# Feed-forward of a two-block layer on one core: ScalarE multiplies the modulation weights in place, GpSimd only adds

## The reference

```python
mod = c_act @ w_ada[l] + b_ada[l]                      # one row of six pieces: sh1, sc1, gt1, sh2, sc2, gt2
...
h = _rmsnorm(x, norm2_g[l]) * (1.0 + sc2) + sh2
x = x + gt2 * _conv_ffn(h, w_up[l], conv_w[l], conv_b[l], w_down[l])     # conv of width 3, silu(gate) * val
...
mod = jnp.einsum('bd,de->be', jax.nn.silu(c), w_ada[layer]) + b_ada[layer]    # second block
```

## Time and profile before

| | |
|---|---|
| median of 3 runs | 3269.93 us (3267.48 to 3271.69) |
| the profiled execution's own time | 3266.9 us |
| its span | 3265.1 us |
| feed-forward in the span | about 1011 to 1844 us |
| PE busy in the span | 2618.0 us (80%) |
| DVE busy | 2094.0 us (64%) |
| ACT busy | 1069.4 us (33%) |
| POOL busy | 672.6 us (21%), all but a little of it in the feed-forward |

### The profile page before, as it was taken

The page is one execution under the profiler, slowest core; times in us unless marked ns, Lnnn a source line. Parts: engine busy times, 40 slices in busy tenths (PEclk is TensorE's granted clock), DMA queues, the critical chain, the costliest instruction groups (busy, mean ns, idle before and its releaser), DMA issues.

```text
span 3265.1 us, 50408 instructions
## 1 busy us (share of the span) xinstructions
PE 2618.0 (80%) x22384; PEld 2536.3 (78%) x22384; DVE 2094.0 (64%) x2395; ACT 1069.4 (33%) x1155; POOL 672.6 (21%) x371
## 2 busy tenths in 40 slices
PE   1189911149497999999999659999999999999986
PEld 1179901149496999999999548999899999999986
DVE  5736488874546888777788645555644576576443
ACT  1133210012233333333333244434433344344332
POOL 0000000000005887887888200000000000000000
PEclk6589955569698999999999879999999999999998
DMA  7746558830256677677777325555466665666653
GB/s 258 241 118 182 160 173 286 288 123 4 62 155 169 208 225 232 212 223 235 226 232 233 103 58 142 143 158 148 137 185 186 181 168 166 183 161 163 181 157 102
DMA packets 757608, 568.64 MB, mean 174 GB/s; under 512 B 45680, under 2 KB 643824, under 8 KB 757264
## 3 DMA queue, kind: packets, MB, share of 16 engines
q1 hardware_dynamic: 756624, 562.40, 59.1%
q0 software_dynamic: 768, 3.02, 0.3%
HBM read 563.29 MB, written 2.10 MB: 173 GB/s over the span
## 4 chain that ended last, share of the span: by engine, by line
PE 71%; DVE 20%; issue 3%; ACT 3%; POOL 1%; DMA 1%; SPq 0%; DVEq 0%; ACTq 0%; POOLq 0%
PE bank L556 19%; PE bank L558 19%; PE bank L557 19%; DVE acc L1309 9%; PE bank L733 2%; PE bank L546 2%; PE bank L610 1%; PE bank L584 1%; PE bank L586 1%; PE bank L585 1%; DVE ez L1713 1%; DVE w_low L1269 1%; DVE hid_low L1607 1%; ACT hf L1003 1%; PE bank L775 1%
## 5 line engine op out<-in xcount | busy, mean ns | idle before, releaser
L556 PE MATMUL bank<-act_high,w_high 128*128 128x256 f32 x4608 | 1314.7, 285 | 123.5 <-issue 56.4
L557 PE MATMUL bank<-act_low,w_high 128*128 128x256 f32 x4608 | 1309.3, 284 | 0.0
L558 PE MATMUL bank<-act_high,w_low 128*128 128x256 f32 x4608 | 1309.0, 284 | 0.0
L1269 DVE TENSOR_TENSOR w_low<-ring,w_high 128x2048 fp32r<-128x2048 f32 x388 | 933.6, 2408 | 433.0 <-ACT w_high L973 426.1
L556 PEld LDWEIGHTS bank<-act_high,w_high 128*128 128x128 f32 x4608 | 888.3, 193 | 128.5 <-issue 59.6
L973 ACT ACTIVATE w_high<-ring 128x2048 fp32r<-128x2048 f32 x388 | 737.6, 1903 | 477.3 <-DMA ring<-w_up 235.9
L557 PEld LDWEIGHTS bank<-act_low,w_high 128*128 128x128 f32 x4608 | 888.4, 193 | 0.1
L558 PEld LDWEIGHTS bank<-act_high,w_low 128*128 128x128 f32 x4608 | 887.9, 193 | 0.1
L515 POOL TENSOR_SCALAR prod<-adf,cact 128x512 f32<-128x512 f32 x165 | 362.9, 2199 | 54.7 <-DMA adf<-w_ada 39.5
L546 PE MATMUL bank<-con,acc 128*128 128x1 f32 x288 | 57.1, 319 | 345.5 <-DVE small L1314 345.5
L546 PEld LDWEIGHTS bank<-con,acc 128*128 128x128 f32 x288 | 55.3, 286 | 348.7 <-DVE small L1314 348.7
(11 more groups left out here) (370 smaller groups left out, 2821.4 us busy)
## 6 DMA issues: line engine op xcount, KB each, us to landing
ring<-w_in SPq DMA_DIRECT2D x182, 1024.0 KB, 5.8
ada<-w_ada SPq DMA_DIRECT2D x100, 1024.0 KB, 5.1
ring<-w_up SPq DMA_DIRECT2D x88, 1024.0 KB, 6.0
adf<-w_ada SPq DMA_DIRECT2D x44, 1024.0 KB, 8.1
ring<-w_down SPq DMA_DIRECT2D x44, 1024.0 KB, 5.0
ring<-w_out SPq DMA_DIRECT2D x16, 1024.0 KB, 6.1
ring<-w_mla SPq DMA_DIRECT2D x16, 1024.0 KB, 5.2
ring<-w_o SPq DMA_DIRECT2D x16, 1024.0 KB, 6.0
```

Of the source, the lines that this page charges most:

```text
L556: pe.matmul(o, wh, ah, start=first, stop=False, skip_group_check=True)
L557: pe.matmul(o, wh, al, start=False, stop=False, skip_group_check=True)
L558: return pe.matmul(o, wl, ah, start=False, stop=last, skip_group_check=True)
L1269: v.tensor_tensor(WL[s][:, 0:WIDE[n]], ring[s][:, 0:WIDE[n]], f32(WH[s][:, 0:WIDE[n]]), ALU.subtract)\
```

## The change

ScalarE multiplies each row tile of a quarter in place, in the `adf` buffer, two tiles behind each up unit's copy: tiles 0 and 1 of quarter q behind up 2q+2 (behind its silu), tiles 2 and 3 behind up 2q+3; those of quarter 3 behind up 0 and up 1 of the next iteration. A new semaphore `f_scaled` counts tiles. GpSimd waits for a quarter's four tiles and then only adds: the first two tiles plus the last two (1024 columns at once), then the two halves, then into the accumulator. It still signals `f_free` when it is done. `prod2` is gone.

```diff
+        f_scaled = sem("f_scaled")
...
                 for q in range(4):
                     k = 4 * turn + q
-                    pool.wait_ge(f_landed[k % 2], 16 * (k // 2 + 1))
-                    w = AF[k % 2][:, :].rearrange("p (j n) -> p j n", j=4)
-                    for j in range(4):
-                        c = (0 if turn < 4 else DT) + 4 * q + j
-                        col = cact[:, c:c + 1]
-                        if q == j == 0:
-                            ins = pool.tensor_scalar(acc[:, :], w[:, j, :], col, None, ALU.mult)
-                        else:
-
-                            pool.tensor_scalar(prod2[:, :], w[:, j, :], col, None, ALU.mult).then_inc(pool_seq, 1)
-                            pool.wait_ge(pool_seq, B.up("pool_seq"))
-                            ins = pool.tensor_tensor(acc[:, :], prod2[:, :], acc[:, :], ALU.add)
...
+                    pool.wait_ge(f_scaled, 4 * (k + 1))
+                    w = AF[k % 2]
+                    pool.tensor_tensor(w[:, 0:1024], w[:, 0:1024], w[:, 1024:2048], ALU.add).then_inc(pool_seq, 1)
+                    pool.wait_ge(pool_seq, B.up("pool_seq"))
+                    if q:
+                        pool.tensor_tensor(w[:, 0:512], w[:, 0:512], w[:, 512:1024], ALU.add).then_inc(pool_seq, 1)
+                        pool.wait_ge(pool_seq, B.up("pool_seq"))
+                        ins = pool.tensor_tensor(acc[:, :], w[:, 0:512], acc[:, :], ALU.add)
+                    else:
+                        ins = pool.tensor_tensor(acc[:, :], w[:, 0:512], w[:, 512:1024], ALU.add)
+                    ins.then_inc(f_free, 1)
+                    pool.wait_ge(f_free, k + 1)
...
+            def scaled(k, js):
+
+                turn, q = divmod(k, 4)
+                act.wait_ge(f_landed[k % 2], 16 * (k // 2 + 1))
+                for j in js:
+                    w, c = AF[k % 2][:, 512 * j:512 * j + 512], (0 if turn < 4 else DT) + 4 * q + j
+                    act.activation(w, w, ACT.Copy, scale=cact[:, c:c + 1]).then_inc(f_scaled, 1)
+
             for i in range(12):
                 for k in range(8):
...
                     if k % 2 == 0 and (k or i):
                         finish()
+                    if 8 * i + k >= 2 and 4 * i + k // 2 - 1 < 44:
+                        scaled(4 * i + k // 2 - 1, (0, 1) if k % 2 == 0 else (2, 3))
```

More of the change, by code:

```diff
@@ L210, in program @@
         acc2 = [at(f"acc2{b}", W0 + 106 + 2 * b, [P, 512]) for b in range(2)]
-        prod2 = at("prod2", W0 + 70, [P, 512])
         BH = at("mix_high", W0 + 32, [P, 8, T], F32R)
```

## The result

The changed kernel takes 3526.45 us (median of 4 runs, 3519.26 to 3527.59), the kernel before 3268.7 us in the same series: a ratio of 1.078, 95% interval 1.077 to 1.080. The forecast was slower, 3487 us, range 3445 to 3525; the direction and the mechanism hold, and the measured median lies 1.5 us past the upper end. The profiled execution took 3525.5 us, 258.6 us more than that of before.

What follows compares the result with a forecast made beforehand. PE was taken to set the pace. Nine iterations at +20.3 us (183 us), +13 us in the first period and +21 us in the last made 217 us on 3266.9, 3484, plus 3 for the median: 3487 us, range 3445 to 3525.

Steps and rivals of the forecast that it cites:

- The walk: One feed-forward iteration step by step from up 3's end as 0: 94.8 us against 74.5, +20.3 us, nine times.
- quarter 2 issued: On SP's queue: quarter 2's load goes at 5.8 us, after quarter 0's adds, up 6's and up 7's loads right behind.
- PE's first wait: Before up 6: PE could begin at 11.5 us but `w_low` is ready at 20.2, a wait of 8.7 us.
- quarter 3 issued: On SP's queue: quarter 3's load goes at 29.6 us, after quarter 1's adds, the next up 0 and up 1 behind.
- PE's second wait: Before the next up 0: PE is done at 34.4 us, `w_low` comes at 43.9, a wait of 9.5 us.
- half clock after it: After the second wait PE starts at the lower clock level, 1.2 GHz in place of 2.4: 2.7 us charged.
- wait before the first down unit: PE's wait for `hid_low`: shorter than the present 3.1 us because `w_low` is no longer slow, 1.3 us.
- The first period: The stretch up to the first of the nine iterations, 81.5 us before, shorter by what it already lost: +13 us.
- the last: The last iteration: down unit at 51.6 us after up 3 in place of 30.8, its weights behind quarter 3: +21 us.
- The wide add: GpSimd's add of 1024 columns: taken as 2.6 us, within bounds of 1.28 and 2.6 us.
- Faster: Rival: the `hid_low` wait (36.0 us) and its half clock (19 us) go, SP's delay is covered: 3212 us, 4 in 100.
- Worse: Rival: up 6 lands with up 7 and POOL's adds each fall behind a `w_low`, 27 us: 3560 us, 7 in 100.

Runs made afterwards that it cites:

- Runs 1, 3 and 4: The changed kernel with, in turn: quarter loads later on SP's queue (3302.64 us), multiplies one pair of units sooner (3297.52 us), a third quarter buffer (3305.68 us).
- Run 7: The changed kernel with one GpSimd wait added, so quarters 2 and 3 are added beside the down units: 3458.83 us, ratio 1.059.
- b_no_pool_work: The kernel before the change with GpSimd's multiplies and adds left out: 3211.13 us, ratio 0.983.
- a_late_defer: The changed kernel with quarter loads later on SP's queue and GpSimd's adds of quarters 2 and 3 beside the down units: 3234.11 us, ratio 0.990.
- a_no_adds: The changed kernel with GpSimd's adds left out and both orders kept: 3359.03 us, ratio 1.029.

## Why the prediction was right, and where its sum was off

**The mechanism** was that quarter 2's and quarter 3's loads wait on SP's in-order queue for a buffer that ScalarE's late multiplies keep from GpSimd, with the weights of up 6, up 7 and the next up 0 and up 1 behind them. Runs 1, 3 and 4 take that wait away in three ways and get 221 to 229 us back.

**The walk**, from up 3's end (1527.8 in the iteration shown), forecast and measured:

| step | forecast | measured |
|---|---|---|
| quarter 2 issued | 5.8 | 5.8 |
| from its issue to the split of up 6 | 10.0 | 8.8 |
| PE's first wait | 8.7 | 7.3 |
| quarter 3 issued | 29.6 | 28.0 |
| from its issue to the split of the next up 0 | 10.0 | 8.8 |
| PE's second wait | 9.5 | 8.3 |
| up 0 begins | 43.9 | 41.1 |
| half clock after it | 2.7 | 1.7 (its copy came at 1576.42, 7.5 us later) |
| wait before the first down unit | 1.3 | 5.9 |
| half clock after that | 0 | 2.3 (1588.07 to 1596.15) |
| the iteration | 94.8 | 98.0 (mean of nine: 98.6) |

The copies of up 3 at 1134.59 and 2022.05 us are nine iterations apart: 98.6 us each, +24.1 in place of +20.3, nine times 217 us. The first period cost 17.2 (1134.59 - 1117.42; forecast 13) and the last 22.5 us (the down unit at 2075.40, 53.4 after its up 3, against 30.8; forecast 21). Together 257 of the 258.6 us between the two profiled executions.

**The step that failed** is the last point of the walk: "a wait before the first down unit. That one gets shorter, since `w_low` is no longer slow and was done long ago: 1.3 us". It became 5.9 us with 2.3 us of half clock, 6.9 us more than forecast and past the 3.5 us that its range allowed, while all up to up 0's begin was 2.8 us shorter and the half clock after it 1.0 us. These errors pull against each other, so that 3487 us came as near as it did in part by luck: with the rest of the walk exact, 6.9 us in each of ten iterations would have made it some 70 us too low. The chain of waits ahead of that unit, in the changed kernel:

```profile
1572.94 2.67 DVE hid_low L1611
...
1575.63 1.28 DVE sil L1599
...
1576.93 1.48 DVE sil L1600
...
1582.66 0.43 DVE hfu L1606
...
1585.33 2.61 DVE hid_low L1611
1587.93 0.14 issue
1588.07 0.55 PE bank L550
```

and what GpSimd did in that time:

```profile
1572.90 2.41 POOL L508 TENSOR_TENSOR adf<-adf 128x1024 f32<-128x1024 f32 x1 [17.12 <-ACT adf L1112]
1575.39 1.36 POOL L511 TENSOR_TENSOR adf<-adf 128x512 f32<-128x512 f32 x1
1576.83 1.30 POOL L513 TENSOR_TENSOR acc<-adf,acc 128x512 f32<-128x512 f32 x1
1585.29 2.35 POOL L508 TENSOR_TENSOR adf<-adf 128x1024 f32<-128x1024 f32 x1 [7.17 <-ACT adf L1112]
```

Each of these two wide adds begins 0.04 us before a `hid_low`. GpSimd is released by ScalarE's last two multiplies, which end at 1572.76 and 1585.15 us; `hid_low` stands behind a `w_low` that ends 0.3 us after them, just too late, and takes 2.6 us where alone it takes 0.42. The loss is 2.2 + 0.9 + 1.0 + 2.2 = 6.3 us for an iteration. Run 7 shows it: with the adds elsewhere 67.6 us come back.

I had looked at `w_low`, the long instruction, and not at the short ones in the chain, though the trace of the kernel before has them. Its DVE and POOL timelines ahead of the down unit of the earlier trace rows:

```profile
1590.31 1.51 DVE L1607 TENSOR_TENSOR hid_low<-hfu,hid_high 128x256 fp32r<-128x256 f32 x1
...
1598.65 1.40 DVE L1602 TENSOR_TENSOR hfu<-sil,cva 128x256 f32<-128x256 f32 x1
```

```profile
1589.21 2.33 POOL L517 TENSOR_TENSOR acc<-prod,acc 128x512 f32<-128x512 f32 x1
...
1594.82 3.49 POOL L515 TENSOR_SCALAR prod<-adf,cact 128x512 f32<-128x512 f32 x1
1598.39 1.38 POOL L517 TENSOR_TENSOR acc<-prod,acc 128x512 f32<-128x512 f32 x1
```

`hid_low` and `hfu` each lost 1 us there, beside an add of 512 columns. An add twice as wide, released next to them, was the term to price.

**Single costs.** A multiply of ScalarE is listed with 0.71 us and the next begins 0.61 us later (two take 1.32), as taken. The wide add took 2.46 us on average, forecast 2.6. An estimate from the figure of the Trainium skill's GPSIMD Engine Reference, section 3.1, was 2.3 us; the shortest here took 2.34, so it was nearer to an add that meets nobody.

**The rivals.** "Faster" had its size right (b_no_pool_work: -56 us) and its condition wrong for this kernel, as forecast. "Worse" named as its second half that GpSimd's adds would each wait for a `w_low`. They hardly waited (2.46 us on average against 2.34 at least); it was the other way round, VectorE's short instructions waited for the adds, and that was in no rival.

## What to carry to other kernels

When work on a shared buffer is handed from one engine to another, follow the buffer's release to the queue that waits for it, and see what stands behind that wait in the queue: here ScalarE, idle for over 60% of the feed-forward, cost most of the 258 us by where its multiplies stood in program order; the same multiplies one pair of units (11.5 us) sooner gave 229 us back. When a chain of short instructions leads to the bound engine, look at what its shared partner does at those moments, not at its busy share: GpSimd's work fell by two thirds, and PE's usual wait behind it almost doubled, until one semaphore put its adds where nobody waited.

## What the runs showed of the hardware

An add of GpSimd shuts out more of VectorE than I had taken from the trace of before: a tensor_scalar of 256 columns (`sil`, L1599) took 1.28 us in place of 0.41, and in a_late_defer, where it met the start of a wide add, 2.66 us. GpSimd is shut out too: in the kernel before a multiply that began at 1594.82 us, 1.2 us into a `w_low`, took 3.49 us in place of 1.6, though a `w_low` that began behind a multiply lost only 0.37 us. The Trainium skill, SBUF — State Buffer, section "SBUF: two separate sides", names both kinds: VectorE's instructions with two SBUF inputs and those in a mode that uses both ports. These rows of `hid_low` and `sil` agree, but none shows in which mode `sil` ran.

Short waits of PE cost more than their length: one of 5.93 us was followed by a down unit of 8.1 us in place of 5.76 (granted clock 0.60 in its first 5.8 us), one of 8.28 us by an up unit of 7.5 us (0.71), while after a wait of 0.87 us in a_late_defer the clock was 1.00 and the unit kept 5.76 us. And three transfers of 1 MB that are issued one right behind the other brought their second one after 8.8 us in the changed kernel, 10.0 us in the first iteration of before and in a_no_adds.
